# Twelve small vector loads move from SyncE's queue to ScalarE's, and their turning moves behind the third input tile

## What is computed

```python
h = concatenate([meta, x])
for i in range(4):
    y = rmsnorm(h, norm_mix_g[i])
    # i = 0, 3: pool_mixer; i = 1: diff_attention; i = 2: conformer_conv
    h = h + mixer(y)
    h = h + swiglu_ffn(rmsnorm(h, norm_ffn_g[i]), w_gate[i], w_up[i], w_down[i])
return rmsnorm(h[:, 16:], final_norm_g)

def pool_mixer(h, w, b, scale):      # windows 2, 4, 8, 16, one for each 256 channels
    pooled = trailing_mean(h_group, window) - h_group
    return (pooled @ w_group + b) * scale
```

## Time and profile before

| | |
|---|---|
| runs | 2036.44, 2040.78, 2040.9 us |
| median | 2040.78 us |
| the profiled execution, its own time | 2036.12 us |
| its span | 2034.4 us |
| TensorE matmul busy | 1993.6 us, 98% of the span |
| VectorE, ScalarE, GpSimd busy | 77%, 44%, 11% |
| mean granted TensorE clock | 0.991 |

### The profile page before, as it was taken

One profiled execution on the slowest core, in us unless ns is written; L12 is line 12 of the kernel. 1 busy time (PEld: TensorE's weight loads), 2 busy tenths in 40 slices (PEclk: granted clock), 3 DMA queues, 4 the chain that ended last, 5 costly groups with the idle time before them and its releaser, 6 DMA issues.

```text
span 2034.4 us, 40286 instructions
## 1 busy us (share of the span) xinstructions
PE 1993.6 (98%) x15908; PEld 1935.3 (95%) x15908; DVE 1570.6 (77%) x2221; ACT 896.5 (44%) x1415; POOL 227.4 (11%) x337
## 2 busy tenths in 40 slices
PE   7999999999998999999999999999999989999998
PEld 7999999999997999999999999999999988989997
DVE  6797778767876688877868886697788758977794
ACT  6443334345554444433457755343344334433342
POOL 5000000322211200000051102000000250000000
PEclk9999999999999999999999999999999989999999
DMA  5423343332211324233336631233343322333332
GB/s 166 137 84 104 88 118 84 94 116 63 62 53 42 94 84 125 78 89 102 109 100 141 133 86 54 90 97 91 95 124 84 115 63 83 96 105 91 101 104 94
DMA packets 304528, 195.22 MB, mean 96 GB/s; under 512 B 7354, under 2 KB 297147, under 8 KB 304148
## 3 DMA queue, kind: packets, MB, share of 16 engines
q1 hardware_dynamic: 298972, 175.08, 30.0%
q0 software_dynamic: 4240, 14.09, 3.2%
q10 hardware_dynamic: 1192, 4.34, 0.6%
HBM read 179.45 MB, written 6.44 MB: 91 GB/s over the span
## 4 chain that ended last, share of the span: by engine, by line
PE 87%; DVE 5%; issue 3%; ACT 2%; POOLq 1%; DVEq 1%; DMA 0%; SPq 0%; POOL 0%; ACTq 0%
PE ps L934 42%; PE ps L1198 34%; PE ps L1051 2%; PE ps L1309 2%; PE ps L992 1%; DVE w_lo L2190 1%; PE ps L1035 1%; PE ps L1381 1%; PE ps L1422 1%; POOLq L813 1%; POOLq L810 1%; PE ps L961 0%; PE ps L1446 0%; PE ps L948 0%; DVE w_lo L2429 0%
## 5 line engine op out<-in xcount | busy, mean ns | idle before, releaser
L1198 PE MATMUL ps<-t_lo,y_hi 128*128 128x264 f32 (+1 forms) x1008 | 285.7, 283 | 0.0
L1198 PE MATMUL ps<-t_lo,w_hi 128*128 128x264 f32 (+1 forms) x1008 | 285.7, 283 | 0.0
L1198 PE MATMUL ps<-t_hi,w_lo 128*128 128x264 f32 (+1 forms) x1008 | 285.4, 283 | 0.0
L1198 PE MATMUL ps<-t_hi,y_lo 128*128 128x264 f32 (+1 forms) x1008 | 285.3, 283 | 0.0
L1198 PE MATMUL ps<-t_hi,w_hi 128*128 128x264 f32 (+1 forms) x1008 | 285.1, 283 | 0.1
L1198 PE MATMUL ps<-t_hi,y_hi 128*128 128x264 f32 (+1 forms) x1008 | 284.8, 283 | 0.0
L1837 ACT ACTIVATE w_hi<-w_raw 128x1024 fp32r<-128x1024 f32 (+1 forms) x108 | 127.8, 1201 | 329.1 <-PE ps L934 193.0
L934 PE MATMUL ps<-hid_hi,w_hi 128*128 128x264 f32 (+1 forms) x1184 | 265.2, 296 | 0.6 <-DVE hid_lo L2485 0.6
L934 PE MATMUL ps<-hid_lo,w_hi 128*128 128x264 f32 (+1 forms) x1184 | 264.7, 296 | 0.0
L934 PE MATMUL ps<-hid_hi,w_lo 128*128 128x264 f32 (+1 forms) x1184 | 264.2, 296 | 0.0
L934 PE MATMUL ps<-y_hi,w_hi 128*128 128x264 f32 (+1 forms) x1088 | 243.8, 300 | 4.9 <-DVE q L2721 1.7
(11 more groups left out here) (350 smaller groups left out, 4372.2 us busy)
## 6 DMA issues: line engine op xcount, KB each, us to landing
w_raw<-in_ffn_w_gate SPq DMA_DIRECT2D x88, 512.0 KB, 5.0
w_raw<-in_ffn_w_up SPq DMA_DIRECT2D x88, 512.0 KB, 4.7
w_raw<-in_ffn_w_down SPq DMA_DIRECT2D x70, 512.0 KB, 4.3
w_raw<-in_ffn_w_down SPq DMA_DIRECT2D x24, 384.0 KB, 4.4
w_raw<-in_attn_w_qkv SPq DMA_DIRECT2D x16, 512.0 KB, 3.8
w_raw<-in_conv_w_in SPq DMA_DIRECT2D x16, 512.0 KB, 4.2
w_lo<-w_raw POOLq DMA_DIRECT2D x16, 512.0 KB, 5.1
w_raw<-in_attn_w_qkv SPq DMA_DIRECT2D x16, 256.0 KB, 2.8
```

What stands on the lines that cost most here:

```text
L1198: mm = pe.matmul(ps[:, bank, 0:hw], w[:, at:at + P], b[:, t, k, 0:hw], start=k == 0 and n == 0, stop=k == 3 and n == 2)
```

## The change

SyncE no longer waits on `vec_zeroed` and no longer issues the twelve vector transfers: the four transfers of `pool_w` follow the input tiles at once. ScalarE's queue does that wait and issues the twelve transfers ahead of everything else in its program. TensorE turns the vectors behind the third tile (`i == 2`) instead of behind the fifth, with a semaphore of its own, `vec_turned`, and VectorE copies them to `vec` behind its copies of the third tile.

```diff
@@ sync
                 sp.dma_start(m.x_rows[0:n, i, :], a["x"][0, t:t + n, :]).then_inc(x_in[i], 16)
-            sp.wait_ge(s.vec_zeroed, 1)
-            for row, name in ((ROW_MIX, "norm_mix_g"), (ROW_FFN, "norm_ffn_g"), (ROW_POOL_B, "pool_b"),
-                              (ROW_POOL_S, "pool_scale"), (ROW_DWB, "conv_dw_b"), (ROW_LNG, "conv_ln_g"),
-                              (ROW_LNB, "conv_ln_b"), (ROW_CONV_OUT, "conv_b_out")):
-                n = a[name].shape[0]
-                sp.dma_start(m.vec_rows[row:row + n, :], a[name]).then_inc(s.vec_in, 16)
-            sp.dma_start(m.vec_rows[ROW_CONV_IN:ROW_CONV_IN + 2, :],
-                         a["conv_b_in"].rearrange("o (r n) -> (o r) n", r=2)).then_inc(s.vec_in, 16)
-            for t, n in ((0, 16), (16, TAPS - 16)):
-                sp.dma_start(m.vec_rows[ROW_DW + t:ROW_DW + t + n, :], a["conv_dw_w"][0, t:t + n, :]).then_inc(s.vec_in, 16)
-            sp.dma_start(m.vec_rows[ROW_SUBLN:ROW_SUBLN + 1, 0:P], a["attn_subln_g"]).then_inc(s.vec_in, 16)
@@ tensor
                 mm.then_inc(s.rows_turned, 1)
-            pe.wait_ge(s.vec_in, 16 * 12)
-            for d in range(NB):
-                mm = pe.transpose(ps[:, 7, d * ROWS:(d + 1) * ROWS], m.vec_rows[:, d * P:(d + 1) * P],
-                                  m.ident[0:ROWS, 0:ROWS])
-            mm.then_inc(s.rows_turned, 1)
+                if i == 2:
+                    pe.wait_ge(s.vec_in, 16 * 12)
+                    for d in range(NB):
+                        mm = pe.transpose(ps[:, 7, d * ROWS:(d + 1) * ROWS], m.vec_rows[:, d * P:(d + 1) * P],
+                                          m.ident[0:ROWS, 0:ROWS])
+                    mm.then_inc(s.vec_turned, 1)
@@ scalar
+            act.wait_ge(s.vec_zeroed, 1)
+            ... the same twelve transfers, issued by act ...
             act.wait_ge(s.tok_cleared, 1)
@@ vector
                 if i < TILES - 1:
                     e.then_inc(s.turned_read, 1)
+                if i == 2:
+                    dve.wait_ge(s.vec_turned, 1)
+                    dve.tensor_copy(m.vec[:, :], ps[:, 7, 0:NB * ROWS]).then_inc(s.vec_ready, 1)
             e.then_inc(s.h_ready, NB)
-            dve.wait_ge(s.rows_turned, TILES + 1)
-            dve.tensor_copy(m.vec[:, :], ps[:, 7, 0:NB * ROWS]).then_inc(s.vec_ready, 1)
             dve.drain()
```

More of the change, by code:

```diff
@@ L358, in __init__ @@
         self.vec_zeroed = sem("vec_zeroed")
+        self.vec_turned = sem("vec_turned")
         self.vec_ready = sem("vec_ready")
@@ L2070, in attention_step @@
                         split_hi(first["attn_out"] + NB + c, 0, 0, 512)
+            act.wait_ge(s.vec_zeroed, 1)
+            for row, name in ((ROW_MIX, "norm_mix_g"), (ROW_FFN, "norm_ffn_g"), (ROW_POOL_B, "pool_b"),
+                              (ROW_POOL_S, "pool_scale"), (ROW_DWB, "conv_dw_b"), (ROW_LNG, "conv_ln_g"),
+                              (ROW_LNB, "conv_ln_b"), (ROW_CONV_OUT, "conv_b_out")):
+                n = a[name].shape[0]
+                act.dma_start(m.vec_rows[row:row + n, :], a[name]).then_inc(s.vec_in, 16)
+            act.dma_start(m.vec_rows[ROW_CONV_IN:ROW_CONV_IN + 2, :],
+                          a["conv_b_in"].rearrange("o (r n) -> (o r) n", r=2)).then_inc(s.vec_in, 16)
+            for t, n in ((0, 16), (16, TAPS - 16)):
+                act.dma_start(m.vec_rows[ROW_DW + t:ROW_DW + t + n, :], a["conv_dw_w"][0, t:t + n, :]).then_inc(s.vec_in, 16)
+            act.dma_start(m.vec_rows[ROW_SUBLN:ROW_SUBLN + 1, 0:P], a["attn_subln_g"]).then_inc(s.vec_in, 16)
             act.wait_ge(s.tok_cleared, 1)
```

## The result

The changed kernel took 2043.71 us in the median of 9 runs (2040.25 to 2045.01), the kernel before 2036.44 us in 9 runs beside it (2035.46 to 2040.9). The ratio is 1.0025, with a 95% interval of 1.0016 to 1.0034. The forecast was 2040.1 us, with a range of 2034.5 to 2042.3: by the ratio the change made the kernel some 5 us slower, and the median lies 1.4 us above the range. What was forecast is a gain of 0.7 us, taken off 2040.78 us, the median of three runs of the kernel before. Its nine runs here came to 2036.44, so 2040.1 lies nearer to the measured time than the mechanism deserves. The profiled execution took 2042.69 us, its span is 2041.0 us and its mean granted clock 0.987, against 2036.12, 2034.4 and 0.991 before.

The account below looks back on a forecast made before the run. TensorE, busy 98% of the span, was taken as the bound, so only an earlier start of its pool matmuls could pay: -0.89 + 0.2 = -0.7 us off the 2040.78 us median gave 2040.1 us, range 2034.5 to 2042.3.

Parts of the forecast that it names:

- the landing of the vectors: DMA engines: last vector transfer, issued at about 5.4 us, lands at 9, bounds 7.4 to 11.3; TensorE wants it by 10.1.
- The bound of 5.94 us: DMA engines: issue to landing of the earlier trace's last vector transfer, behind the whole input, used for the landing's late bound.
- the weights are late next, no change: Third rival, pool weights: same bytes ahead, first lands at about 13.4 as before; 2040.8 us, -0.3 to +0.3, chance 0.18.
- The vectors land late and TensorE stands before tiles four and five: Second rival, TensorE's wait at `i == 2`: start 0.8 us later; 2041.6 us, bounds +0.1 and +1.5, chance 0.12.
- `h_ready` at L + 3.34: Late-vectors rival: after landing L come transposes 0.7, fourth tile 0.9, copies 1.27 and 0.47; chance 0.12.
- Contention on the input tiles, 0.2 us: DMA engines: vectors take engine time from the input tiles, delaying the start of squares, transposes and copies by 0.2 us.
- the two prices given: ScalarE's queue: twelve issues from 1.75 end at 5.65 us at SyncE's price or 6.4 at ScalarE's, starting it 0.3 or 1.0 later.
- the 11.5 taken: DMA engines: pool weights, issued from 3.64, land between 9.8 and 13.4 us, taken as 11.5; ScalarE's squares last until 12.3.
- The dip to 166 GB/s: DMA engines at 9 to 10 us: full share at 166 GB/s against 340 either side, taken to speak for slack.
- The 2.99 us from `h_ready` to the pool: VectorE's own work before the first pool matmul: 2.99 us from `h_ready` at 13.64 gives a start at 16.63, 0.89 earlier.
- clock comes back earlier: First rival, pool matmuls on TensorE: granted clock stays up or rises sooner; 2038.1 us, bounds -1.7 and -4, chance 0.15.
- -0.7 us on the start: Sum for the kernel's start: -0.89 from the earlier `h_ready` plus 0.2 for contention, carried through to the end; chance 0.48.

Follow-up runs that it names:

- alone: Changed kernel with twelve vector semaphores, SyncE waiting until all vectors landed before issuing the first input tile; taps took 2.0 us from issue to landing, one execution.
- fill_after: Changed kernel with 28 unread identity transposes ahead of TensorE's vector wait and 30 ahead of the pool; 2042.51 us, 1.0018.
- act_only: Kernel before with both queues as in the change, but the vectors turned behind the fifth tile as before; 2039.68 us, 1.001.
- turn_only: Kernel before with SyncE's old order, only the vectors' turning and copy moved behind the third tile; 2040.26 us, 1.001.
- weights_first: Kernel before with all transfers on SyncE, pool weights ahead of the vectors, turning behind the fifth tile; 2040.51 us, 1.0012.
- fill_late: Kernel before with 24 unread identity transposes on TensorE ahead of the pool only; 2038.01 us, 0.9997.
- few: Changed kernel with twelve semaphores, the five single-row vector transfers left out; vectors turned at 12.22 us against 13.55, one execution.
- no_taps: Changed kernel with twelve semaphores, the two taps transfers left out; vectors turned at 12.64 us against 13.55, one execution.
- spread: Changed kernel with twelve semaphores, each single row sent as 16 pieces to unread rows; vectors turned at 12.84 us against 13.55, one execution.
- held: Changed kernel with SyncE waiting until all twelve vectors have landed before it issues the pool weights; 2039.4 us, 1.0008.
- swdge: Kernel before with the five single-row vector transfers issued by GpSimd behind the identity instead of by SyncE; 2039.89 us, 1.001.

## Why the prediction was wrong

**The step that failed is the landing of the vectors.** The prediction took 9 us, from bounds of 7.4 to 11.3, where TensorE wanted them at 10.1. They landed at 13.32, past either bound. The reasoning was that the input would no longer stand ahead of them. But the input and the vectors run on the same engines, and beside it the last vector takes 7.55 us from issue where it takes under 2 alone (`alone`: last issue at 5.62, all twelve landed when the first input tile was issued at 7.38). The bound of 5.94 us from the earlier trace rows was read as a time that follows an issue; it was the time until the engines were through with what they had. The landing of before, 13.17, would have been the better guide, and it was in the same row.

**The rivals had the mechanism and a part of the price.** The third, "the weights are late next, no change" (0.18), said that the landings of the same bytes don't move, and that held within 0.2 us for the vectors and the first weight and within 0.6 for the last. Its "no change" did not: the wait had moved ahead of two tiles, while the landing had not. The second is the one whose place was right. "The vectors land late and TensorE stands before tiles four and five" had a chance of 0.12 and the formula `h_ready` at L + 3.34. With L = 13.32 this is 16.66; `h_ready` came at 18.06. The 1.4 us between are the low clock: 0.4 on the turning of the vectors and 1.2 on the last tiles (`fill_after` has 0.70 and 1.70 us for them, the changed kernel 1.09 and 2.94), less what VectorE overlapped. With the clock up the formula holds: in `fill_after` `h_ready` came 3.47 us behind the landing. The rival's upper bound of +1.5 us was therefore too low: +2.1 by its own formula with the measured L, and +3.5 with the clock.

**Contention on the input tiles, 0.2 us, was the second term mis-sized.** It was looked for at the first tile, and that one did land in time (TensorE began at 5.26, before at 5.45); but the third landed 1.1 us later and the fourth 2.9, at 12.5. With the prediction's own durations that tile alone puts `h_ready` at 12.5 + 0.9 + 1.27 + 0.47 = 15.1 and the pool at 18.1, an estimate: even with the vectors there at 9 the change would have lost. `act_only`, whose fourth tile landed at 11.8, measures it as a pool start of 18.43, 0.9 later than before.

**Right, or harmless:** ScalarE's issues took 1.79 to 6.04, between the two prices given, and pushed its table load from 5.38 to 6.13. The first weight landed at 13.6 instead of the 11.5 taken, and nobody waited for it, since ScalarE's squares, held by the fourth tile, ended at 14.7. The dip to 166 GB/s had been read as slack; it stands in the changed kernel too (163 GB/s at a share of 1.06 from 9 to 10 us), and the weights came no earlier. The 2.99 us from `h_ready` to the pool were exact. The rival "clock comes back earlier" went the other way at first: one long pause at 10 us made the clock fall 4 us sooner. The 120 matmuls then took 0.35 us less than before.

**The shape of the whole.** The forecast set -0.7 us on the start; it was +3.5. The later stages added between -0.5 and +3.0 in the two profiles of the changed kernel (from the column of 587 us to the last). A loss of 3.6 us is 1.0018, inside both measured intervals, [1.0016, 1.0034] and [1.0001, 1.0021]. That the first measurement lay higher through later falls of the clock fits its one profile; for the other runs it isn't shown.

**What stays open.** That `fill_after` is slower than the kernel before by 1.0018 with a pool that ends only 0.24 us later may mean that something reaches beyond the start, or only that its profiled execution, 2038.98 us, was one of the faster of its runs. One profile for each kernel can't separate an effect of the start on the later falls of the clock, near 40 us in `turn_only` and `weights_first` above all, from chance; the same holds for `fill_late`, whose 2.8 us at the start don't show in its ratio. Nor is it settled what a small transfer costs an engine that is busy with the input: `few`, `no_taps` and `spread` give 1.3, 0.9 and 0.7 us in one execution each. Why the fourth tile comes 2 to 3 us later when the small transfers go through a second queue is argued from `held` and `spread` and not shown engine by engine. And no order tried made the start earlier than that of the kernel before without filling TensorE's pauses.

## What to carry to other kernels

Moving a small transfer to an idle queue moves its issue, not its landing, when a large transfer occupies the engines: forecast the landing from when the engines are through, and put the wait for it where the landing of the old kernel already lies, never ahead of work whose data are there. Where TensorE is the bound, price a new stall twice, once for the stall and once for the clock that falls with it, and take off the second what the old stalls cost in clock already.

## What the runs showed of the hardware

- Twelve transfers of 0.5 to 64 KB beside 2 MB of input landed 7.55 us after the last issue, alone at most 1.8 us after it. The earlier issue on ScalarE did not bring the moment forward: 12.7 to 13.2 us in three kernels that issue them on SyncE behind the input (before, `turn_only`, `fill_late`), 13.1 to 13.5 in five that issue them on ScalarE.
- The small transfers also delayed the large ones more when issued from another queue: the fourth input tile landed at 9.6 before and at 12.5 after, and at 10.5 with five of the small ones issued by GpSimd (`swdge`).
- The issue of a small transfer took 0.25 to 0.4 us on SyncE, 0.27 to 0.57 us on ScalarE, and 0.49 to 0.70 us on GpSimd.
- A pause of 1.6 us on TensorE left the granted clock at 1.00 in `fill_late`, where TensorE was then kept busy; after one of 1.69 us it fell in `turn_only`, 1.3 us after the work had begun again; one of 3.4 us brought it to 0.50 within the pause (changed kernel). Transposes of a constant that nobody reads kept it at 1.00 in three kernels, and 120 matmuls took 14.3 instead of 16.5 to 16.8 us.
- Two of the kernels with such filling had executions of 3924 and 4986 us among 22, at a mean clock of 1.0. Their cause is unknown.
